# Dilated attention heads of a two-block transformer kernel: value products with the values stationary, in pairs on column halves, and outputs kept turned

## What the reference computes

```python
def dilated_attention(q, k, v, positions):
    h = N_HEADS_C
    q = partial_rope_2(to_heads(q, h), positions)
    k = partial_rope_2(to_heads(k, h), positions)
    v = to_heads(v, h)
    outs, lses = [], []
    for window, dil in DILATED_PATTERNS:
        o, lse = dilated_branch(q, k, v, window, dil)
        outs.append(o)
        lses.append(lse)
    wts = jax.nn.softmax(jnp.stack(lses, axis=0), axis=0)
    o = jnp.sum(wts[..., None] * jnp.stack(outs, axis=0), axis=0)
    return from_heads(o)
```

## Time and profile before

| | us |
|---|---|
| median of three runs | 2212.37 |
| the three runs | 2210.89, 2212.37, 2212.39 |
| span of the profiled execution | 2210.5 |

### The profile page before, as it was taken

How to read it: one execution, slowest core, us unless ns; L and a number is a source line. 1 busy time by engine, 2 the same in 40 slices (tenths; PEclk the granted TensorE clock), 3 DMA queues, 4 the chain that set the end, 5 groups by cost and what they waited for, 6 DMA issues and landing times.

```text
span 2210.5 us, 33160 instructions
## 1 busy us (share of the span) xinstructions
PE 2158.2 (98%) x12377; PEld 1842.0 (83%) x12377; DVE 1498.9 (68%) x2234; ACT 946.0 (43%) x1891; POOL 1195.8 (54%) x594
## 2 busy tenths in 40 slices
PE   6999999999999999999999999999999999999997
PEld 4788888877899988887887898888897887889886
DVE  6834777554666592897646777677996727777676
ACT  3254663011556510544743555512545725455412
POOL 4747403776477677745016654577653037544675
PEclk9999999999999999999999999999999999999999
DMA  8322102522133233222002222322322002222221
GB/s 323 153 77 89 55 30 84 190 89 96 58 115 107 105 140 133 93 105 86 1 1 95 96 78 113 113 95 79 113 81 75 1 32 84 86 106 115 95 95 57
DMA packets 32776, 206.78 MB, mean 94 GB/s; under 512 B 4080, under 2 KB 4336, under 8 KB 11632
## 3 DMA queue, kind: packets, MB, share of 16 engines
q1 hardware_dynamic: 32192, 200.27, 24.8%
q10 hardware_dynamic: 432, 4.46, 0.5%
HBM read 202.61 MB, written 2.10 MB: 93 GB/s over the span
## 4 chain that ended last, share of the span: by engine, by line
PE 88%; DVE 6%; issue 1%; ACT 1%; DMA 1%; DVEq 1%; POOL 1%; POOLq 0%; SPq 0%; ACTq 0%
PE PS L1126 18%; PE PS L1128 18%; PE PS L1127 18%; PE PS L1605 5%; PE PS L1617 5%; PE PS L1382 3%; PE PS L1381 3%; PE PS L1383 3%; PE PS L1631 3%; PE PS L1457 2%; PE PS L1459 2%; PE PS L1458 2%; PE PS L1256 1%; PE PS L1259 1%; PE PS L1258 1%
## 5 line engine op out<-in xcount | busy, mean ns | idle before, releaser
L665 POOL TENSOR_TENSOR w_hi<-raw,zero_c 128x512 fp32r<-128x512 f32 (+1 forms) x135 | 281.6, 2104 | 545.5 <-PE PS L1128 544.3
L669 POOL TENSOR_TENSOR w_lo<-raw,w_hi 128x512 fp32r<-128x512 f32 (+1 forms) x135 | 365.0, 2723 | 5.8
L1126 PE MATMUL PS<-b_hi,w_hi 128*128 128x512 f32 x512 | 203.1, 397 | 0.9 <-POOL w_lo L888 0.9
L1127 PE MATMUL PS<-b_lo,w_hi 128*128 128x512 f32 x512 | 203.0, 396 | 0.0
L1128 PE MATMUL PS<-b_hi,w_lo 128*128 128x512 f32 x512 | 203.0, 396 | 0.0
L3345 DVE TENSOR_TENSOR b_lo<-a_all,b_hi 128x512 fp32r<-128x512 f32 x44 | 162.6, 3733 | 49.3 <-ACT b_hi L2490 49.3
L1126 PE MATMUL PS<-f_hi,w_hi 128*128 128x512 f32 x448 | 177.6, 397 | 0.7 <-DVE f_lo L2647 0.7
L1128 PE MATMUL PS<-f_hi,w_lo 128*128 128x512 f32 x448 | 177.6, 396 | 0.0
L1127 PE MATMUL PS<-f_lo,w_hi 128*128 128x512 f32 x448 | 177.6, 396 | 0.0
L688 POOL TENSOR_TENSOR w_lo<-raw,w_hi 128x512 fp32r<-128x512 f32 x48 | 70.9, 1477 | 92.9 <-ACT w_hi L2482 92.9
L1126 PEld LDWEIGHTS PS<-b_hi,w_hi 128*128 128x128 f32 x512 | 96.4, 188 | 24.6 <-POOL w_lo L888 1.1
(11 more groups left out here) (586 smaller groups left out, 6868.7 us busy)
## 6 DMA issues: line engine op xcount, KB each, us to landing
raw<-slabs_dram SPq DMA_DIRECT2D x161, 1024.0 KB, 4.8
aux<-ada_dram SPq DMA_DIRECT2D x18, 512.0 KB, 5.7
ada_first<-ada_dram SPq DMA_DIRECT2D x11, 512.0 KB, 14.1
cmpw<-cmpw_dram ACTq DMA_DIRECT2D x2, 2048.0 KB, 12.7
ada_late<-ada_dram SPq DMA_DIRECT2D x8, 512.0 KB, 3.2
ada_last<-ada_dram SPq DMA_DIRECT2D x8, 512.0 KB, 6.4
xT<-xT_dram SPq DMA_DIRECT2D x1, 2048.0 KB, 9.3
out_dram<-t SPq DMA_DIRECT2D x4, 512.0 KB, 3.2
```

The source lines that it names most:

```text
L665: high = nc.gpsimd.tensor_tensor(w_hi[:, slot, c], raw[:, slot, c], zero[:, 0:c.stop - c.start], ALU.add)
L669: low = nc.gpsimd.tensor_tensor(w_lo[:, slot, c], raw[:, slot, c], w_hi[:, slot, c].bitcast(f32), ALU.subtract)
L1126: nc.tensor.matmul(out, a_hi_, b_hi_, start=start, stop=False)
L1127: nc.tensor.matmul(out, a_hi_, b_lo_, start=False, stop=False)
```

## The change

In the dilated heads the roles of the two operands are swapped. The turned probabilities of a pair of heads are copied, unscaled, into `wide_pT`, where all queries of one block of 128 keys lie side by side. When both heads of a pair are done, `wide_values` multiplies them in eight matmuls: the 64 columns of a head's values are stationary, the turned probabilities of key block b (512 - 128 b columns) stream, and the first head's output goes to partitions 0 to 63 and the second's to 64 to 127 of one bank. The outcome is the pair's output already turned, so `o2_transpose` is not done for it. Since queries now lie along the columns, the inverse row sums have to lie there too: DVE takes the reciprocals of the pair's sums, POOL spreads them over 128 columns (`spread`), PE transposes them into bank 3, ACT copies them to `wide_by`, and DVE multiplies the output by it in PSUM (`o2_scale`). Then ACT and DVE form `o_hi` and `o_lo` from that bank.

The pairs are done at steps 63, 71 and 79, and the last one inside the first slab of `w_out`, after its bank 0. The order of the eight turns and of that slab's banks changes. `O2` holds only the plain and differential heads (its offsets change). The dilated heads' copies no longer wait for a value product, and `finish` is not run for them. The block from `class Place` to `o2_splits` is moved ahead of the GpSimd program, since `spread` uses names of it; some semaphores are merged (`cmpw_loaded`, the `cmp_` ones, `c_copied_` into `c_taken_`).

```diff
+        wide_pT = [at("wide_pT0", 108544, [P, TT, SEQ]), T2[:, 0:4, :], T2[:, 8:12, :], at("wide_pT3", 40960, [P, TT, SEQ])]
+        wide_inv = stats[:, 224:232].rearrange("p (g j) -> p g j", g=2)
+        wide_rows = at("wide_rows", 120832, [P, TT, 2, HD])
+        wide_by = at("wide_by", 118784, [P, SEQ])
...
@@ Plan
-                    self.pvs.setdefault(turn + 2, []).append(v)
-                    self.takes.setdefault(turn + 3, []).append(v)
-                self.steps = turn + 4
+                    if not self.is_wide[v]:
+                        self.pvs.setdefault(turn + 2, []).append(v)
+                        self.takes.setdefault(turn + 3, []).append(v)
+                self.steps = turn + (1 if self.is_wide[-1] else 4)
...
-        O2_TURNS = [(56, 4, 3), (59, 5, 7), (63, 0, 10), (67, 6, 8), (70, 7, 8), (73, 1, 12), (80, 2, 14)]
+        O2_TURNS = [(56, 4, 3), (59, 5, 7), (63, 0, 7), (67, 6, 8), (71, 1, 8), (75, 7, 8), (79, 2, 8), (83, 3, 8)]
+        def o2_bank(i):
+            return PS[:, 3, :] if i >= 4 else PS[:, 6 + i % 2, :]
+        def wide_slot(jb, j, nb):
+            return wide_pT[jb["wide"] % 4][:, 0:nb, 128 * j:128 * j + 128]
...
@@ GpSimd
+            def spread(layer):
+                for pair in range(4):
+                    pool.wait_ge(wide_inv_ready, 4 * layer + pair + 1)
+                    nc.gpsimd.tensor_copy(wide_rows[:], wide_inv.rearrange("p g j -> p j g").unsqueeze(3)
+                                          .to_broadcast([P, TT, 2, HD])).then_inc(wide_spread, 1)
...
                         at = input_low(INPUTS[layer])
+                        run(at, at + 2)
+                        spread(layer)
+                        at += 2
...
@@ PE
+            def wide_values(pair, copied):
+                at_.wide += 1
+                pe.wait_ge(wide_spread, at_.wide)
+                for j in range(TT):
+                    last = nc.tensor.transpose(PS[:, 3, 128 * j:128 * j + 128],
+                                        wide_rows[:, j, :, :].rearrange("p g d -> p (g d)"), ident)
+                last.then_inc(wide_turned, 1)
+                for ready in (copied_act, copied_dve):
+                    pe.wait_ge(ready, max(count for s_, count in copied if s_ is ready))
+                for b in range(TT):
+                    for g in (0, 1):
+                        h = 2 * pair + g
+                        last = nc.tensor.matmul(PS[64 * g:64 * g + 64, 6 + pair % 2, 128 * b:512],
+                                                z2[:, 5, b, 64 * h:64 * h + 64], wide_pT[h % 4][:, b, 128 * b:512],
+                                                start=b == 0, stop=b == TT - 1, skip_group_check=True)
+                last.then_inc(turned, 1)
...
                 def o2_transpose(n):
-                    _, i, maps = O2_TURNS[n] if n < KD - 1 else (0, 3, 16)
+                    _, i, maps = O2_TURNS[n]
                     pe.wait_ge(out_used, m0 + maps)
+                    if n > 0 and O2_TURNS[n - 1][1] < 4:
+                        pe.wait_ge(wide_copied, at_.wide)
+                    else:
+                        pe.wait_ge(turned_dve, base + n)
+                    if i < 4:
+                        if i >= 2:
+                            pe.wait_ge(turned_dve, base + o2_order.index(i - 2) + 1)
+                        wide_values(i, [copies_2[v] for v in plan_2.pair_values[i]])
+                        return
...
                 def last_turn(b):
-                    if b == 2:
+                    if b == 0:
                         o2_transpose(KD - 1)
...
-                              bank_ready=o2_banks, order=(0, 1, 2, 4, 5, 6, 7, 3), after=last_turn)
+                              bank_ready=o2_banks, order=(0, 1, 2, 4, 5, 6, 3, 7), after=last_turn)
...
@@ ACT
+                        if plan.is_wide[v]:
+                            A(wide_slot(jobs[m], j, nb), bank.rearrange("p (b q) -> p b q", b=nb), ACT.Copy
+                              ).then_inc(copied_act, 1)
+                            continue
...
+                def wide_copy():
+                    at_.wide += 1
+                    act.wait_ge(wide_turned, at_.wide)
+                    A(wide_by[:], PS[:, 3, :], ACT.Copy).then_inc(wide_copied, 1)
...
+                    for n, (at_step, i, _) in enumerate(O2_TURNS[:-1]):
+                        if step == at_step and i < 4:
+                            wide_copy()
+                        if step == at_step + (2 if i < 4 else 1):
+                            o2_high(n, i)
...
@@ DVE
+                    for pair, i in plan.pair_end.items():
+                        if step == i + WIDE_INV_LAG:
+                            of = plan.sums[plan.scores[i][0] - 1][0] % 8
+                            dve.wait_ge(probs_ready, g0 + i + 1)
+                            V.reciprocal(wide_inv, rowsum[:, of:of + 2, :]).then_inc(wide_inv_ready, 1)
...
+                def o2_scale(n, i):
+                    if i < 4:
+                        at_.scaled += 1
+                        dve.wait_ge(turned, at_.turn + n + 1)
+                        dve.wait_ge(wide_copied, at_.scaled)
+                        V.tensor_tensor(o2_bank(i), o2_bank(i), wide_by[:], ALU.mult).then_inc(wide_scaled, 1)
...
+                    if step - 1 in o2_step:
+                        n = o2_step[step - 1]
+                        o2_scale(n, O2_TURNS[n][1])
+                    for n, (at_step, i, _) in enumerate(O2_TURNS[:-1]):
+                        if step == at_step + (3 if i < 4 else 2):
+                            o2_low(n, i)
```

More of the change, by code:

```diff
@@ L645, in _, with __init__ @@
             sp.wait_ge(stored, 16 * KD // 2)
+        class Place:
+            def __init__(self):
+                self.meets = self.slab = self.drain = self.norms = self.bank = 0
+                self.tile = self.value = self.map = self.pair = self.acopies = self.dcopies = 0
+                self.turn = self.turn_a = self.turn_d = self.part = self.ffn = self.conv = 0
+                self.x = self.free = self.pairs = self.roots = self.mixes = self.folds = 0
+                self.narrow = self.wide = self.scaled = 0
@@ L900, in _ @@
                     pool.drain()
[L903 to L960, removed]
-                self.slots, self.before, last = [], [], {}
-                self.masks, self.masked_before, last_mask = [], [], {}
-                taken = {"pair": 0, "beside": 0, "alone": 0}
-                for i, (m, c, j, woven) in enumerate(self.scores):
-                    kind = "pair" if is_pair(jobs[m]) else "beside" if woven else "alone"
-                    base, size = {"pair": (0, P_PAIRS), "beside": (P_PAIRS, 2), "alone": (0, P_SLOTS)}[kind]
-                    slot = base + taken[kind] % size
-                    taken[kind] += 1
-                    self.slots.append(slot)
-                    self.before.append(last.get(slot))
-                    last[slot] = value_of[m, j]
-                    slot = i % (M_SLOTS + 1 if woven else M_SLOTS)
-                    self.masks.append(slot)
-                    self.masked_before.append(last_mask.get(slot))
-                    last_mask[slot] = i
-                self.turns, self.pvs, self.takes = {}, {}, {}
-                turn, at_step = 0, []
-                for v, t in enumerate(self.values):
-                    turn = max(turn, due[t])
-                    if v >= PT_SLOTS + PT_BANKS:
-                        turn = max(turn, at_step[v - PT_SLOTS - PT_BANKS] + 3)
-                    at_step.append(turn)
-                    self.turns.setdefault(turn, []).append(v)
-                    self.pvs.setdefault(turn + 2, []).append(v)
-                    self.takes.setdefault(turn + 3, []).append(v)
-                self.steps = turn + 4
@@ L1590, in attend @@
                         copies.append((copied_act, a))
+                return copies, a, d
+            def attend(jobs, ring, s_banks=S_BANKS, banks_ready=None, also=None, fill=FILL):
+                plan = Plan(jobs)
+                g0, v0, m0, p0 = at_.tile, at_.value, at_.map, at_.pair
+                (copies, a, d), joined = value_copies(jobs, plan), []
+                for m, j, _ in plan.values:
                     at_.pair += is_pair(jobs[m])
@@ L1940, in _ @@
                 at_.turn_d += KD
[L1941 removed]
+                order = o2_order
                 def o2_banks(b):
```

397 lines of the change are left out of this document (239 added, 158 removed).

## The result

The changed kernel takes 2218.95 us (median of seven runs, 2217.01 to 2220.31), the kernel before 2212.39 beside it (seven runs): a ratio of 1.003 with an interval of 1.002 to 1.0041. It is slower by 0.3%, as forecast, and both the sign and the size (2220.5) held. The medians differ by 6.6 us; the profiled execution of the changed kernel is the slowest of its seven (2220.31). The experiments show that the size came out partly by chance: two terms were too high, and one that made up for them was not in the sum at all.

A forecast was written before the change was run, and what follows sets the result against it. PE was taken as the bound, 98% busy at full clock; -5.0 us of PE work and +9.2 of waits gave +4.2 a layer, +8.4 in all, forecast 2220.5 us. Range for 8 in 10: 2209 to 2237.

The forecast's parts named there:

- PE's own work: Dilated heads, per layer: value products removed (16.2 us), wide matmuls of four pairs added (11.2 us), net -5.0 us.
- the lump: A pair's eight wide value matmuls on PE, halves beside each other, one record behind: 2.60 us plus 0.20 for shape changes.
- The waits: PE waits in the dilated heads that removed value products had covered, or new ones: 10.6 us for 1.4, +9.2 a layer.
- the five waits behind the 384-column score: Heads 3 to 7: transposes wait for the chain score, mask, exponential, copy; 0.72 us each, 3.6 a layer.
- Three behind the 256-column score: In three heads an `o_hi` ahead of an exponential delays the next copy by 0.6 us each, 1.8 a layer.
- the long one: Transpose of step 67 waits behind DVE's scaling of the differential heads at step 64: 3.1 us a layer.
- the turn at step 59: This turn waits for the remainder of step 56, which PE now reaches sooner: 0.7 us a layer.
- the early heads: Waits of the kernel before in the first and second dilated heads that stay: 0.8 us a layer.
- wait for POOL: Last lump waits for POOL's spread, mostly covered by bank 0 of the `w_out` slab: 0.6 us stays.
- One behind the other: Rival: a pair's two heads run serially on PE, 4.34 us plus 0.20 a pair, total 2234.8 us; chance 0.27.
- Faster: Rival: ACT and DVE run ahead during the lump, chain waits stay hidden, only -5.0 a layer remains, 2202.4 us; chance 0.12.
- No difference: Rival: pairs wholly parallel and waits two thirds of the sum, -7.5 + 6.5, within 0.2%; chance 0.06.

The follow-up runs named there:

- the filler's kernel: Changed kernel plus three 512-column products of constants, result unread, on TensorE at step 67 ahead of the waiting transposes; 2217.35 us, ratio 1.0023 to the kernel before.

## Why the prediction was right, and where it was not

**What bounds the kernel**: right. PE's path decided; DVE and ACT had time on the whole and were late at places.

**PE's own work**: too pessimistic, -5.0 for -6.2. The mis-sized term is the lump, "2.17 + 0.43 = 2.60 us a pair" and 0.20 for the change of shape. It measured 2.30, with 0.11 more on the next score (1110.76 - 1109.79 = 0.97 for 0.86): the second half is not one record behind the first but beside it. I also took the sums' turns as equal to those removed; one is 1107.49 - 1106.96 = 0.53 for 0.44. So 4 x (2.30 + 0.11 + 0.09) = 10.0 in place of 11.2. (Two slips of the working change nothing: the sum for a head is 5.74, not 5.73, and two thirds of the +9.2 are 6.1, not the 6.5 of the last rival.)

**The waits**: right in kind and nearly in sum. With the clock at full speed (the filler's kernel) the five waits behind the 384-column score lose 0.75, 0.76, 0.65, 0.75 and 0.66, 3.6 in all (forecast 3.6). Three behind the 256-column score lose 1.7 (1.8), the long one 3.35 (3.1), the turn at step 59 0.75 (0.7), the early heads 1.05 (0.8). At the last lump no wait for POOL appeared (0.6 forecast): the spread takes 0.62 us, just under the lower end of its term, half of 1.32; 0.3 was lost at the last head's transposes instead. Sum 10.7, forecast 10.6. I set 1.4 against it for the kernel before, from its wait view; counted from start to start it lost 2.1.

So at full clock the stage should have grown by -6.2 + 10.7 - 2.1 = 2.4 us a layer, and it did: 66.11 - 63.58 = 2.5. By the forecast's own terms, rightly sized, the kernel would have come out 5 us slower, not 8.

**What was missing**: the clock. I read the page of the kernel before as full speed throughout, and let a wait cost its own length only. But the page gives the clock of each slice of 55 us as one digit in tenths, a 9 throughout, and that hides a short fall; only the mean of 0.996 hints at one. Ahead of its last 6.2 us the trace of the kernel before has three stretches of 3.41 us at half clock, all outside the changed stage. One follows a wait of 2.67 us:

```profile
954.76 0.39 PE L1256 MATMUL PS<-w_hi,ys_hi 128*128 128x256 f32 x1 [2.67 <-DVE w_lo L3447]
```

```profile
955.06:958.47 3.41, 3.41 (x18) 3.41 (x17) 3.41 (x4) 0.00 (x0) 1.30 (x1) 0.50 0.00 0
```

The others begin at 228.02 us, behind waits of 0.61 and 1.17, and at 1596.76, behind one of 1.90. So the price of a long wait could have been read there with the clock in it: in the stretch shown, records of 256 columns start 0.21 us apart, and 0.12 at full clock. In the changed kernel the 3.35 us wait also halved the clock, at a cost of 1.5 and 1.8 us in the profiled execution. That filled the gap to 4.0 and 4.3 a layer, beside a forecast of 4.2: the closeness of the two is luck.

**The rivals.** One behind the other: refuted by the lump, and the kernel with the halves in sequence shows its price, 3.85 us a lump, not 4.34. Faster, because ACT and DVE run ahead in the lump: wrong as the kernel stands, for DVE idles through it. But its condition, that the waits be hidden, can be brought about in part: with DVE's scaling in the lump and the copies first the kernel is 0.2% faster than before. No difference: its wholly parallel pairs came true, its waits, two thirds of my sum, did not.

## What to carry to other kernels

Work that is taken from the bounding engine may have been the cover of a chain on other engines: write down the chain beside the work between its ends before counting the saving, and then give the chain's links the slots that the new layout opens (here the lump, in which DVE idles). Matmuls on two column halves overlap if they are issued in turn; issued in sequence, only the records at the seam do. A long wait of TensorE can cost half as much again behind it through the clock (here 1.5 to 1.8 us behind 3.35, but 0.7 in one case), so read the granted clock beside the waits, in short stretches, and break the longest first.

## What was not expected of the hardware

- The granted clock fell to 1.2 GHz for 3.41 or 6.82 us at the long wait in the eight stages that had it, and stayed at 2.4 in the stages where the wait was gone or held filler.
- Records on the two halves start within 0.01 us of each other, and four matmuls (eight records) of each half take 2.30 us together, where one head's scores of the same widths take 2.17.
- A record for the other half overtook the last three of the busy one (1108.94 before 1109.15 and 1109.47).
- POOL's copy of 128x512 with a broadcast input is twice as fast as its subtraction of that size. The row of that line in the changed kernel (duration ns, least, median and most):

```profile
L1041 POOL COPY wide_rows<-stats x8: 611/617/618, 1099.3 to 1794.3; 128x512 f32<-128x512 f32 x8
```
